# A two-model forward pass in float32: the dense feed-forwards with weight columns stationary

## The chip, the core and the metric

The kernel runs on one core of a Trainium2 chip. Five engines work side by side, each through its own instructions in order, and wait for one another by semaphores: TensorE (PE; its weight loads are listed apart as PEld), VectorE (DVE), ScalarE (ACT), GpSimd (POOL) and SyncE (SP), which here starts the weight transfers. The metric is the device time of one execution in microseconds (us). Before the change it is 2497.68 us, the median of three runs (2497.55 to 2498.68).

## What is computed

256 tokens of width 1024 go through two small models of two layers each. Every layer is a mixer (attention and recurrences, merged by gates) and a feed-forward. Three of the four feed-forwards are dense, with 2816 hidden channels; the last is a mixture of 8 experts. The change touches the dense ones alone:

```python
def rms_norm(x, g):
    xf = x.astype(jnp.float32)
    y = xf * lax.rsqrt(jnp.mean(xf * xf, axis=-1, keepdims=True) + NORM_EPS)
    return (y * g.astype(jnp.float32)).astype(x.dtype)

def swiglu(h, w_in, w_out):                  # layers 0 and 1 of the first model
    gate, up = jnp.split(h @ w_in, 2, axis=-1)
    return (jax.nn.silu(gate) * up) @ w_out
...
        h = rms_norm(x, ln2[l])
        x = x + swiglu(h, w_ffn_in[l], w_ffn_out[l])

def swiglu_2(h, w1, w3, w2):                 # layer 0 of the second model
    return (jax.nn.silu(h @ w1) * (h @ w3)) @ w2
```

## The kernel before

**Products in float32 out of rounded halves.** TensorE multiplies rounded numbers here (type fp32r). So each weight and each activation is split into its rounded value and the remainder, and a product is made of three: rounded by rounded, remainder of x by rounded weight, rounded x by remainder of the weight. All weights (616 MB) stream from memory in chunks of 128 x 2048 (1 MB). For every chunk ACT writes the rounded copy (`conv`, L1461, tile `w_hi`, a ring of 3 slots) and DVE the remainder (`conv`, L1917, tile `w_lo`, in place of the raw chunk, a ring of 6). PE counts `w_used` up when it is through with a chunk; ACT rounds chunk c only once chunk c-3 is used up, and SP fetches chunk c once chunk c-6 is.

**The dense feed-forward** (`feed_forward`) runs over J = 11 blocks of 256 hidden channels. A block takes three chunks: two for the up products (`up`, eight k tiles of 128 in two halves, each with 256 gate and 256 up columns) and one for the down product (`down`). In `up`, a k tile of x for 128 tokens is stationary and 512 weight columns move (`gemm_half`, L792 to L794: three products for each of 4 k tiles and 2 token tiles, 24 of 512 columns in a chunk). The result has tokens on the partitions: one of the eight PSUM banks for each token tile, gate columns left and up columns right. Blocks alternate between banks 0, 1 and banks 2, 3 (`gbank`). ACT takes the silu of the gate half (scaled per token by the norm's factor, column 4+t of `nstat`), DVE multiplies it by the up half (L2441, `gprod`). The down product contracts over hidden channels, which must then lie on the partitions, so PE turns `gprod` by four transposes of 128 x 128 for each block (`turn_block`, L774), ACT rounds the turned values (`ghi`) and DVE writes their remainder (L2449, `glo`). The down products of all blocks add up in banks 4 to 7, called X.

**The order.** `walk` gives the order for each engine: first up of block 0 (both halves), up of block 1 (first half), turn of block 0, up of block 1 (second half), down of block 0; then for each further block: up (first half), turn of the block before, up (second half), down of the block before. The middle blocks are a hardware loop. In block j = J-2, the last block's turn stands in the middle of the down product.

**The start of a feed-forward.** Before it, the mixer's output product adds up in banks 0 to 3: banks 0 and 1 hold columns 0 to 511 of the update of x, banks 2 and 3 the rest. DVE adds them to x (`add_to_x`, L1952) and so sets them free: 0 and 1 while PE still makes the second half, 2 and 3 after its end. PE transposes x in four norm tiles into the X banks (L774 `x`); ACT rounds them (`xhi`), DVE makes the remainders (L1936, `xlo`). Tiles 0 and 1 are transposed before the first up product, tiles 2 and 3 in its middle (`rest_of_norm`), since they need the second half of x. ACT sums the squares (`hrow`), and computes the factor of the norm only after it has rounded the next chunk (`scale`: two table loads, a logarithm and an exponential).

**Lines to follow**: `up` with `gemm_half` (L792 to L794), `turn_block` (L774), `down` with `gemm_rows` (L807 to L809), `add_to_x` (L1952), `lo_tiles` (L1936), `conv` of ACT (L1461) and of DVE (L1917).

## Time and profile before

| | us |
|---|---|
| median of three runs | 2497.68 |
| the profiled execution | 2497.54 |
| its span, first to last instruction | 2495.9 |
| PE busy with products | 2472.0 (99%) |
| DVE busy | 1814.5 (73%) |
| ACT busy | 1523.7 (61%) |

Busy time of PE is the union of records that overlap: a record of 512 columns lasts 0.39 us, but one starts every 0.227 us, and it is this distance that counts. Shapes in a row are partitions x elements; `x4` counts instructions that stand together. In a timeline, a row gives start, duration, engine, line, operation, and in brackets how long the engine sat idle before it and who ended that.

### The profile page before, as it was taken

Reading aid. Unit: us, or ns where it says so; the run is one execution under the profiler, and the core shown is the slowest. Engines: PE = TensorE matmul, PEld = TensorE weight load, DVE = VectorE, ACT = ScalarE, POOL = GpSimd, SP = SyncE. Lnnn points to the kernel's source line nnn. Section 1 sums busy time; section 2 is a strip of 40 time slices with the busy share of each in tenths; the row PEclk is TensorE's granted clock in tenths of the full one; section 3 lists DMA queues with packets and bytes.
Section 4 is the critical chain, followed back from the end, with each engine's and each line's share of the span. In section 5 each row is a group of like instructions: output and inputs, shape, how many; then the busy total and the mean of one; then the engine's idle time right before and its main releaser. Section 6 shows DMA issues by size and latency. Waiting matters only on the chain.

```text
span 2495.9 us, 31808 instructions
## 1 busy us (share of the span) xinstructions
PE 2472.0 (99%) x11756; PEld 2024.7 (81%) x11756; DVE 1814.5 (73%) x1839; ACT 1523.7 (61%) x1589; POOL 153.5 (6%) x133
## 2 busy tenths in 40 slices
PE   8999999999999999999999999999999999999998
PEld 7888888888888888888888887888888888888877
DVE  6687655657775555665556577989889898998988
ACT  6565544555554455545445546777777777777776
POOL 0102000020020000110000023000000000000010
PEclk9999999999999999999999999999999999999999
DMA  7445555544455564555554456999999999999996
GB/s 262 152 161 177 171 188 190 172 158 152 169 179 190 187 208 161 182 173 186 187 184 169 169 194 252 383 368 387 385 374 385 373 386 375 385 369 392 368 402 254
DMA packets 90684, 633.76 MB, mean 254 GB/s; under 512 B 10462, under 2 KB 10838, under 8 KB 15841
## 3 DMA queue, kind: packets, MB, share of 16 engines
q1 hardware_dynamic: 85584, 616.63, 66.9%
q0 software_dynamic: 4720, 15.57, 1.7%
q8 instruction: 60, 0.98, 0.2%
q10 hardware_dynamic: 288, 0.33, 0.0%
q14 instruction: 32, 0.25, 0.0%
HBM read 625.00 MB, written 7.48 MB: 253 GB/s over the span
## 4 chain that ended last, share of the span: by engine, by line
PE 96%; DVE 2%; ACT 1%; DMA 1%; issue 1%; SPq 0%; ACTq 0%; DVEq 0%
PE bank L792 13%; PE bank L794 13%; PE bank L793 13%; PE bank L1371 8%; PE bank L1373 8%; PE bank L1372 8%; PE bank L1344 4%; PE bank L1346 4%; PE bank L1345 4%; PE bank L774 4%; PE bank L807 4%; PE bank L809 4%; PE bank L808 4%; PE bank L1200 1%; PE bank L1201 1%; PE bank L1199 1%
## 5 line engine op out<-in xcount | busy, mean ns | idle before, releaser
L1917 DVE TENSOR_TENSOR w_lo<-raw,w_hi 128x2048 fp32r<-128x2048 f32 x583 | 1341.6, 2303 | 417.6 <-ACT w_hi L1461 405.5
L1461 ACT ACTIVATE w_hi<-raw 128x2048 fp32r<-128x2048 f32 (+1 forms) x588 | 1120.1, 1907 | 259.9 <-PE bank L809 117.3
L792 PE MATMUL bank<-w_hi,xhi 128*128 128x512 f32 x1456 | 579.9, 398 | 1.5 <-DVE w_lo L1917 0.7
L794 PE MATMUL bank<-w_lo,xhi 128*128 128x512 f32 x1456 | 567.9, 390 | 0.0
L793 PE MATMUL bank<-w_hi,xlo 128*128 128x512 f32 x1456 | 567.5, 390 | 0.0
L1371 PE MATMUL bank<-w_hi,xhi 128*128 128x512 f32 x896 | 358.8, 400 | 0.8 <-DVE w_lo L1917 0.5
L1373 PE MATMUL bank<-w_lo,xhi 128*128 128x512 f32 x896 | 350.0, 391 | 0.0
L1372 PE MATMUL bank<-w_hi,xlo 128*128 128x512 f32 x896 | 349.6, 390 | 0.0
L792 PEld LDWEIGHTS bank<-w_hi,xhi 128*128 128x128 f32 x1456 | 273.4, 188 | 66.3 <-issue 7.5
L794 PEld LDWEIGHTS bank<-w_lo,xhi 128*128 128x128 f32 x1456 | 273.3, 188 | 58.5
L793 PEld LDWEIGHTS bank<-w_hi,xlo 128*128 128x128 f32 x1456 | 273.7, 188 | 53.0
L1373 PEld LDWEIGHTS bank<-w_lo,xhi 128*128 128x128 f32 x896 | 168.2, 188 | 35.5
L1371 PEld LDWEIGHTS bank<-w_hi,xhi 128*128 128x128 f32 x896 | 168.3, 188 | 33.3 <-DVE w_lo L1917 1.3
L1461 ACT ACTIVATE ghi<-bank 128x256 fp32r<-128x256 f32 x178 | 65.0, 384 | 212.1 <-PE bank L774 212.1
L1372 PEld LDWEIGHTS bank<-w_hi,xlo 128*128 128x128 f32 x896 | 168.7, 188 | 31.4
L1344 PE MATMUL bank<-w_hi,ghi 128*128 128x512 f32 x448 | 175.4, 392 | 1.2 <-DVE glo L2526 1.1
L1346 PE MATMUL bank<-w_lo,ghi 128*128 128x512 f32 x448 | 174.5, 389 | 0.0
L1345 PE MATMUL bank<-w_hi,glo 128*128 128x512 f32 x448 | 174.3, 389 | 0.0
L807 PE MATMUL bank<-w_hi,ghi 128*128 128x512 f32 x264 | 103.5, 392 | 0.0
L809 PE MATMUL bank<-w_lo,ghi 128*128 128x512 f32 x264 | 102.8, 389 | 0.0
L808 PE MATMUL bank<-w_hi,glo 128*128 128x512 f32 x264 | 102.8, 389 | 0.0
L2783 POOL TENSOR_TENSOR u<-u,gates 128x512 f32<-128x512 f32 x32 | 61.2, 1944 | 655.0 <-DVE gates L2355 655.0
(371 smaller groups left out, 2307.2 us busy)
## 6 DMA issues: line engine op xcount, KB each, us to landing
raw<-in_wexpert SPq DMA_DIRECT2D x336, 1024.0 KB, 4.9
raw<-in_wdense SPq DMA_DIRECT2D x248, 1024.0 KB, 4.8
expert_rows<-y POOLq DMA_DIRECT2D x7, 512.0 KB, 4.8
expert_rows<-back POOLq DMA_DIRECT2D x3, 512.0 KB, 3.9
x<-in_x SPq DMA_DIRECT2D x2, 512.0 KB, 4.6
raw<-in_wdense SPq DMA_DIRECT2D x4, 256.0 KB, 6.1
biasT<-bias_rows POOLq DMA_DIRECT2D x1, 1024.0 KB, 6.3
normal_rows<-hnorm POOLq DMA_DIRECT2D x1, 1024.0 KB, 8.2
```

Of the source, the lines that this page charges most:

```text
L792: mm(bank[banks[t]][:, :], xhi[:, k0 + k, tok], wh, start=start and k == 0, stop=False)
L793: mm(bank[banks[t]][:, :], xlo[:, k0 + k, tok], wh, start=False, stop=False)
L794: last = mm(bank[banks[t]][:, :], xhi[:, k0 + k, tok], wl, start=False, stop=stop and k == 3)
L807: mm(b, xh, hi[:, h, o:o + 512], start=first and k == 0, stop=False)
L1344: mm(dst, ghi[:, m, j % 2, :], hi[:, h, w], start=first, stop=False)
L1345: mm(dst, glo[:, m, j % 2, :], hi[:, h, w], start=False, stop=False)
L1346: return mm(dst, ghi[:, m, j % 2, :], lo[:, s, w], start=False, stop=final)
L1371: mm(bank[b][:, :], xhi[:, kt, 0:P], hi[:, h, w], start=kt == 0, stop=False)
L1372: mm(bank[b][:, :], xlo[:, kt, 0:P], hi[:, h, w], start=False, stop=False)
L1373: last = mm(bank[b][:, :], xhi[:, kt, 0:P], lo[:, s, w], start=False, stop=kt == KT - 1)
L1461: return nc.scalar.activation(dst, src, f, **kw)
L1917: V.tensor_tensor(lo[:, c % RAW, :], raw[:, c % RAW, :], hi[:, c % HI, :].bitcast(F32), ALU.subtract).then_inc(lo_ready, 1)
```

## The change

The up products are turned round. A 128 x 128 piece of the weights is stationary, and the tokens move: the tiles `xhi` and `xlo` become the two halves of one tile `xboth`, so one product of the rounded weights sees 512 columns (256 tokens rounded, 256 tokens of remainders) and fills a whole bank, and a second product of the weights' remainder sees 256 columns and adds to the bank's left half. Four banks (gate and up, two pieces of 128 channels each) are one block, and all blocks use banks 0 to 3. The result is channel-major at once. The transposes are gone. The two halves of each bank are added by ACT (copy of the right half to `side`) and DVE (sum). The norm's factor is per token, now along the free axis: PE spreads it over the partitions once for each feed-forward (a product of ones with a diagonal, `diag`, into `rstd_row`), and DVE multiplies by it. ACT's silu, DVE's product, ACT's rounding and DVE's remainder follow, all of 128 x 256, out of SBUF.

```diff
-                        for t in range(NT):
-                            claim((k, "U", j), 2 * (j % 2) + t, streamed=True)
-                            claim((k, "T", j), 2 * (j % 2) + t)
+                        claim((k, "U", j), 0, 1, 2, 3, streamed=True)
+                    claim((k, "R"), X[3])
...
+                        kt, w = 4 * half + kk, slice(kk * 512 + (m % 2) * FB + m // 2 * P, kk * 512 + (m % 2) * FB + m // 2 * P + P)
+                        both = bank[m][:, :].rearrange("p (a b) -> p a b", a=2)
+                        if kt < KT - 1:
+                            mm(both, hi[:, h, w], xboth[:, :, kt, :], start=kt == 0, stop=False)
+                            return mm(bank[m][:, 0:S], lo[:, s, w], xhi[:, kt, :], start=False, stop=False)
+                        mm(bank[m][:, 0:S], lo[:, s, w], xhi[:, kt, :], start=False, stop=False)
+                        return mm(both, hi[:, h, w], xboth[:, :, kt, :], start=False, stop=True)
+
+                    if j == 0 and half == 0:
+                        for m in range(4):
+                            pe.wait_ge(free[m], use((k, "U", j), m))
+                        for kk in range(4):
+                            if kk == 2:
+                                rest_of_norm(k)
+                            for m in range(4):
+                                last = channels(m, kk)
+                    else:
+                        for m in range(4):
+                            if half == 0:
+                                pe.wait_ge(free[m], use((k, "U", j), m) + 2 * it)
+                            for kk in range(4):
+                                last = channels(m, kk)
+                            if half == 1 and m == 1:
+                                last.then_inc(first_block_done, 1)
+                    last.then_inc(w_used, 1)
+                    if j == 0 and half == 1:
+                        b = X[3]
+                        pe.wait_ge(free[b], use((k, "R"), b))
+                        pe.wait_ge(diag_ready, DENSE[k] + 1)
+                        for t in range(NT):
+                            last = mm(bank[b][:, t * P:t * P + P], C("ones"), diag[:, t, :], start=True, stop=True)
+                        last.then_inc(full[b], 1)
...
-                    for t in range(NT):
-                        b = gbank(j, t)
-                        pe.wait_ge(free[b], ev((k, "T", j), b) + 2 * it)
+                    pe.wait_ge(glo_done, FFB[k] + 2 * j + 2 + 4 * it)
```

ACT, after each block's up products:

```diff
                     conv(c0 + c + 2, it)
-                        go(silu[:, t, :], bank[gbank(j, t)][:, 0:FB], ACT.Silu, scale=nstat[:, 4 + t:5 + t]).then_inc(silu_done, 1)
+                    for m in range(2):
+                        if m == 0:
+                            act.wait_ge(first_block_done, FFB[k] // 2 + j + 1 + 2 * it)
+                        else:
+                            act.wait_ge(w_used, c0 + c + 1 + 6 * it)
+                        for i in (2 * m, 2 * m + 1):
+                            last = go(side[:, i, :], bank[i][:, S:2 * S], ACT.Copy)
+                        last.then_inc(side_ready, 1)
+                    for m in range(2):
+                        act.wait_ge(gate_scaled, FFB[k] + 2 * j + m + 1 + 4 * it)
+                        go(silu[:, m, :], silu[:, m, :], ACT.Silu).then_inc(silu_done, 1)
```

DVE, after each block's up products (`added` takes two sums out of the banks and frees them, `scaled` multiplies both by `rstd_row`; `products`, in the place of the turn, multiplies gate by up and writes the remainders):

```diff
                     conv(c0 + c + 2, it)
+                    added(0)
+                    if j > 0:
+                        scaled(0)
+                    added(1)
+                    if j == 0:
+                        b = X[3]
+                        wait_full((k, "R"), b)
+                        V.tensor_copy(rstd_row[:, :], bank[b][:, 0:S]).then_inc(free[b], 1)
+                        dve.wait_ge(free[b], ev((k, "R"), b))
+                        scaled(0)
+                    scaled(1)
+                    if j == J - 1:
+                        products(j, it)
```

The order on PE at the first up product of the first dense feed-forward, before and then after; `bank_freeN` is the semaphore by which bank N comes free, L792 and L1286 are the first up products, and `ident_t,x` is a norm transpose:

```order
L792 MATMUL bank<-w_hi,xhi 128x512 [waits bank_free1,lo_ready,bank_free0,bank_free4]
L793 MATMUL bank<-w_hi,xlo 128x512
L794 MATMUL bank<-w_lo,xhi 128x512
...
L774 MATMUL bank<-ident_t,x 128x128 [waits bank_free3,bank_free6,bank_free2,bank_free5]
L774 MATMUL bank<-ident_t,x 128x128 x3
L774 MATMUL bank<-ident_t,x 128x128 [waits bank_free7,bank_free3,bank_free2]
```

```order
L1286 MATMUL bank<-xboth,w_hi 128x512 [waits bank_free1,bank_free2,bank_free0,bank_free3,lo_ready,bank_free4]
L1287 MATMUL bank<-xboth,w_lo 128x256
L1286 MATMUL bank<-xboth,w_hi 128x512
...
L782 MATMUL bank<-ident_t,x 128x128 [waits bank_free3,bank_free6,bank_free2,bank_free5]
L782 MATMUL bank<-ident_t,x 128x128 x3
L782 MATMUL bank<-ident_t,x 128x128 [waits bank_free7,bank_free3,bank_free2]
```

The wait for banks 2 and 3 moved from the middle of the first up chunk to its first product.

The order on PE where block 1 begins, before and then after:

```order
L792 MATMUL bank<-w_hi,xhi 128x512 [waits lo_ready,bank_free3,bank_free2]
...
L774 MATMUL bank<-ident_t,gprod 128x128 [waits bank_free0]
L774 MATMUL bank<-ident_t,gprod 128x128
L774 MATMUL bank<-ident_t,gprod 128x128 [waits bank_free1]
L774 MATMUL bank<-ident_t,gprod 128x128
L792 MATMUL bank<-w_hi,xhi 128x512 [waits lo_ready]
```

```order
L1289 MATMUL bank<-xboth,w_hi 128x512
L1313 MATMUL bank<-diag,cst 128x128 [waits rstd_diagonal_ready,bank_free7]
L1313 MATMUL bank<-diag,cst 128x128
L1286 MATMUL bank<-xboth,w_hi 128x512 [waits bank_free0,lo_ready]
L1287 MATMUL bank<-xboth,w_lo 128x256
...
L1286 MATMUL bank<-xboth,w_hi 128x512 [waits bank_free1]
```

Block 1 waited for banks 2 and 3, which block 0 had not used; now it waits for banks 0 and 1, which block 0 has just filled.

The order on DVE over the same place, before and then after (L1917 and L1955 write the remainder of a weight chunk):

```order
L1917 TENSOR_TENSOR w_lo<-raw,w_hi 128x2048 [waits hi_ready] x2
L2441 SCALAR_TENSOR_TENSOR gprod<-bank,nstat,silu 128x256 [waits silu_done] x2
L1917 TENSOR_TENSOR w_lo<-raw,w_hi 128x2048 [waits hi_ready]
L2449 TENSOR_TENSOR glo<-bank,ghi 128x2x128 [waits gated_hi] x2
```

```order
L1955 TENSOR_TENSOR w_lo<-raw,w_hi 128x2048 [waits hi_ready]
L2524 TENSOR_SCALAR diag<-ident_t,nstat 128x128 [waits norm_rstd]
L2524 TENSOR_SCALAR diag<-ident_t,nstat 128x128
L1955 TENSOR_TENSOR w_lo<-raw,w_hi 128x2048 [waits hi_ready]
L2482 TENSOR_TENSOR silu<-bank,side 128x256 [waits remainder_products_out]
L2482 TENSOR_TENSOR gprod<-bank,side 128x256
L2482 TENSOR_TENSOR silu<-bank,side 128x256 [waits remainder_products_out]
L2482 TENSOR_TENSOR gprod<-bank,side 128x256
L2499 COPY rstd_row<-bank 128x256 [waits bank_full7]
```

The sums that free banks 0 and 1 stand behind the remainder of the chunk after next.

## Rows read from the trace of the kernel before

**Rows 1.** The page: busy time of the engines, and shares of the last chain.
```profile
PE 2472.0 (99%) x11756; PEld 2024.7 (81%) x11756; DVE 1814.5 (73%) x1839; ACT 1523.7 (61%) x1589; POOL 153.5 (6%) x133
PE 96%; DVE 2%; ACT 1%; DMA 1%; issue 1%; SPq 0%; ACTq 0%; DVEq 0%
```

**Rows 2.** Line L774 within 283:470 us: times are min/median/max in ns.
```profile
L774 PE MATMUL bank<-ident_t,gprod x44: 270/272/273, 293.4 to 453.5; 128*128 128x128 f32 x44
```

**Rows 3.** Timeline of PE, loop of the first dense feed-forward.
```profile
299.28 0.39 PE L807 MATMUL bank<-w_hi,ghi 128*128 128x512 f32 x1
...
304.72 0.39 PE L792 MATMUL bank<-w_hi,xhi 128*128 128x512 f32 x1
...
310.16 0.60 PE L774 MATMUL bank<-ident_t,gprod 128*128 128x128 f32 x4
310.52 0.47 PE L792 MATMUL bank<-w_hi,xhi 128*128 128x512 f32 x1
310.83 0.39 PE L793 MATMUL bank<-w_hi,xlo 128*128 128x512 f32 x1
...
450.41 0.39 PE L807 MATMUL bank<-w_hi,ghi 128*128 128x512 f32 x1
```

**Rows 4.** Timeline of PE, start of the first dense feed-forward.
```profile
275.61 0.49 PE L792 MATMUL bank<-w_hi,xhi 128*128 128x512 f32 x1
...
278.49 1.03 PE L774 MATMUL bank<-ident_t,x 128*128 128x128 f32 x8
279.28 0.47 PE L792 MATMUL bank<-w_hi,xhi 128*128 128x512 f32 x1
...
282.36 0.47 PE L792 MATMUL bank<-w_hi,xhi 128*128 128x512 f32 x1
```

**Rows 5.** Timeline of DVE there.
```profile
276.26 1.28 DVE L1952 TENSOR_TENSOR x<-bank,x 128x512 f32<-128x512 f32 x2
...
288.44 2.29 DVE L1917 TENSOR_TENSOR w_lo<-raw,w_hi 128x2048 fp32r<-128x2048 f32 x1 [3.02 <-ACT w_hi L1461]
...
294.61 0.75 DVE L2449 TENSOR_TENSOR glo<-bank,ghi 128x256 fp32r<-128x256 f32 x2
```

**Rows 6.** Timeline of ACT there.
```profile
279.75 1.55 ACT L1461 ACTIVATE xhi<-bank,par 128x256 fp32r<-128x256 f32 x4
...
286.49 1.92 ACT L1461 ACTIVATE w_hi<-raw 128x2048 fp32r<-128x2048 f32 x1
...
293.77 0.66 ACT L1461 ACTIVATE ghi<-bank 128x256 fp32r<-128x256 f32 x2 [1.40 <-PE bank L774]
```

**Rows 7.** Timeline of PE and DVE, the other two dense feed-forwards.
```profile
727.71 0.50 PE L792 MATMUL bank<-w_hi,xhi 128*128 128x512 f32 x1
...
1122.20 0.50 PE L792 MATMUL bank<-w_hi,xhi 128*128 128x512 f32 x1
...
728.35 1.28 DVE L1952 TENSOR_TENSOR x<-bank,x 128x512 f32<-128x512 f32 x2
```

**Rows 8.** Timeline of PE, products of 256 moving columns with 28 stationary ones.
```profile
16.65 0.28 PE L920 MATMUL bank<-xhi,wsm_hi 128*28 128x256 f32 x1
...
17.45 0.28 PE L921 MATMUL bank<-xlo,wsm_hi 128*28 128x256 f32 x1
```

**Rows 9.** Timeline of PEld, loads of 128 columns; L947 moves 256 columns, L948 128.
```profile
44.74 0.19 PEld L947 LDWEIGHTS bank<-tri,zs 128*128 128x128 f32 x1
44.85 0.19 PEld L948 LDWEIGHTS bank<-tri,zs 128*128 128x128 f32 x1
44.97 0.19 PEld L792 LDWEIGHTS bank<-w_hi,xhi 128*128 128x128 f32 x1
...
310.83 0.19 PEld L794 LDWEIGHTS bank<-w_lo,xhi 128*128 128x128 f32 x1
```

**Rows 10.** Windows (length, busy us of the engines, granted clock, DMA share, GB/s); PE's longest idle.
```profile
1525.00:1530.00 5.00, 3.55 (x20) 3.49 (x20) 3.81 (x22) 2.36 (x4) 1.88 (x4) 0.57 1.01 324
...
1524.58 0.36 PE L1438 MATMUL bank<-chosen,cst 128*128 128x8 f32 x2 [2.15 <-DVE chosen L2552]
```

More of the change, by code:

```diff
@@ L595, in program @@
         NEXT = dict(zip(phases, phases[1:]))
+        NORMS = {p: i for i, p in enumerate(p for p in phases if p[0] == "norm")}
+        DENSE = {p: i for i, p in enumerate(p for p in phases if p[0] in ("ffn1", "ffn2"))}
         def gated(j):
@@ L1269, in up @@
                             pe.wait_ge(free[X[i]], ev(("norm", k[1], k[0]), X[i]))
-                    banks = [gbank(j, t) for t in range(NT)]
-                    if half == 0:
-                        for b in banks:
-                            pe.wait_ge(free[b], use((k, "U", j), b) + 2 * it)
-                    gemm_half(banks, c0 + c, 4 * half, half == 0, half == 1, it,
-                              middle=(lambda: rest_of_norm(k)) if j == 0 and half == 0 else lambda: None)
-                def turn(j, it):
-                    if j < J - 1:
-                        turn_block(j, it)
@@ L1796, in up_done, with rounded @@
                     conv(c0 + c + 2, it)
[L1797 to L1799 removed]
+                    for m in range(2):
[10 more added lines that the diff above has]
+                    if j == J - 1:
+                        rounded(j, it)
+                def rounded(j, it):
+                    for m in range(2):
+                        act.wait_ge(product_ready, FFB[k] + 2 * j + m + 1 + 4 * it)
+                        go(gated(j)[0][:, m, :, :].rearrange("p t n -> p (t n)"), gprod[:, m, :], ACT.Copy).then_inc(ghi_done, 1)
                 def turn(j, it):
[L1802 to L1805 removed]
+                    if j < J - 1:
+                        rounded(j, it)
                 walk(act, J, lambda j, it, c: conv(c0 + c + 2, it) if c else None, turn, up_done, lambda j, it, c: conv(c0 + c + 2, it))
@@ L2452, in feed_forward, with added @@
-                walk(dve, J, lambda j, it, c: conv(c0 + c + 2, it), turn, up_done, down)
+                    def added(m):
+                        if f0 + 2 * j + m > 1:
+                            dve.wait_ge(glo_done, f0 + 2 * j + m - 1 + 4 * it)
+                        dve.wait_ge(side_ready, f0 + 2 * j + m + 1 + 4 * it)
+                        for i, dst in ((2 * m, silu), (2 * m + 1, gprod)):
+                            V.tensor_tensor(dst[:, m, :], bank[i][:, 0:S], side[:, i, :], ALU.add).then_inc(free[i], 1)
@@ new lines, in scaled @@
+                    def scaled(m):
+                        for i, dst in ((2 * m + 1, gprod), (2 * m, silu)):
+                            dve.wait_ge(free[i], ev((k, "U", j), i) + 2 * it)
+                            last = V.tensor_tensor(dst[:, m, :], dst[:, m, :], rstd_row[:, :], ALU.mult)
+                        last.then_inc(gate_scaled, 1)
+                    conv(c0 + c + 2, it)
+                    added(0)
+                    if j > 0:
+                        scaled(0)
+                    added(1)
@@ new lines, in up_done, with products @@
+                    if j == 0:
[5 more added lines that the diff above has]
+                    scaled(1)
+                    if j == J - 1:
+                        products(j, it)
+                def products(j, it):
+                    for m in range(2):
+                        dve.wait_ge(silu_done, f0 + 2 * j + m + 1 + 4 * it)
+                        V.tensor_tensor(gprod[:, m, :], gprod[:, m, :], silu[:, m, :], ALU.mult).then_inc(product_ready, 1)
+                    for m in range(2):
+                        dve.wait_ge(ghi_done, f0 + 2 * j + m + 1 + 4 * it)
+                        gh, gl = (part[:, m, :, :].rearrange("p t n -> p (t n)") for part in gated(j))
+                        V.tensor_tensor(gl, gprod[:, m, :], gh.bitcast(F32), ALU.subtract).then_inc(glo_done, 1)
@@ new lines, in turn, with up_begun @@
+                def turn(j, it):
+                    if j < J - 1:
+                        products(j, it)
+                def up_begun(j, it, c):
+                    conv(c0 + c + 2, it)
+                    if j == 0:
+                        dve.wait_ge(norm_rstd, NORMS["norm", k[1], k[0]] + 1)
+                        for t in range(NT):
+                            last = V.tensor_scalar(diag[:, t, :], ident_t[:, :], nstat[:, 4 + t:5 + t], None, ALU.mult)
+                        last.then_inc(diag_ready, 1)
@@ L2454, in pick_first @@
+                walk(dve, J, up_begun, turn, up_done, down)
             def pick_first():
```

40 lines of the change are left out of this document (13 added, 27 removed).

## The prediction

> **What bounds the kernel now.** I read the page first: PE is busy for 99% of the span and makes up 96% of the chain that ended last, DVE and ACT are at 73% and 61% [rows 1]. So time leaves the kernel only if PE gets fewer or closer products, and returns if PE waits. Next I read PE's timeline through the loop of a dense feed-forward. The reader is to see the distance between starts: the down product begins at 299.28 and the next chunk's up products at 304.72, so 24 products of 512 columns take 5.44 us, 0.227 each. The down product of the tenth block begins at 450.41; that is nine periods of (450.41 - 299.28) / 9 = 16.79 us [rows 3]. Three chunks at 5.44 make 16.32. The other 0.47 us is the turn: four transposes from 310.16 to 310.52, and a first product behind them that takes 0.31 before the next starts, with a few slightly longer ones after it [rows 3]. There are 44 transposes, 11 turns, in each feed-forward [rows 2], 33 turns in all three.
>
> **What goes.** All 33 turns. In the steady blocks that is 0.47 us each and nothing hides behind them, because PE has no idle time there. I count them by layer: 10 turns lie after the first down product, 10 x 0.47 = 4.7 us, three times 14.1 us. The first turn is inside the start, which I work out by itself.
>
> **What stays equal.** A chunk had 24 products of 512 columns. Now it has 16 of 512 and 16 of 256, the same 12288 columns. What is unknown is the distance that a 256-column product keeps with a full load of 128 columns behind it; the kernel before has none in steady flow. Lower bound: half of 0.227, 0.113. Near it lie the 256-column products with 28 stationary columns: seven from 16.65 to 17.45, 0.114 each [rows 8]. Upper bound: loads of 128 columns at 44.85 and 44.97, 0.12 apart around a 256-column product, in a stretch right after an interruption; the loads at 44.74 and 44.85, around a product of 128 columns, show that a load alone comes every 0.11 [rows 9]. A load of 0.11 just fits under a product of 0.113. I take 1.2 ns over the lower bound, nearer to the flowing row. There are 16 x 2 x 33 = 1056 such products: +1.3 us, with ends 0 and 1056 x 7.7 ns = +8.1 us. The load must lie beside the running product for this, and it does: the load for L794 and the product L793 both start at 310.83 [rows 3, 9]. The Trainium skill, TensorE: Matmul & The Clock Gate, section "Part 3: Packing small matmuls — row/col tiling", says that a weight load overlaps a running matmul only when the row group differs; here all loads and products use all rows, so the trace disagrees. By that rule the 528 extra loads at its P / 1.2 (an estimate from the page: 107 ns) would add 56 us.
>
> **What is added beside PE.** Each block, DVE now has four sums, four multiplications, two products and two remainders, six pairs. A pair of 256-column operations takes 0.75 us [rows 5], so 4.5 us, with three weight remainders of 2.29 11.4 us out of 16.3. ACT has four copies (two pairs of 0.66 [rows 6]), silu and rounding, 2.7 us, and three roundings of 1.92: 8.4 us. Neither is a bound. In steady flow I count from the start T of a block's second up chunk. DVE is through with the chunk's remainder at T+4.4, frees banks 0 and 1 by T+5.2, ACT's copies of the other two banks end at T+6.3, banks 2 and 3 are free at T+7.1, and PE wants bank 0 at T+10.9. Behind ACT's wait for the scaled gate stands the rounding of the next chunk but one: it starts at about T+8.3, its remainder is done at T+12.5 and PE wants it at T+16.3. In the last block, the chain from the end of the up products to the last remainder (copies, sums, scaling, silu, product, rounding, remainder) is about 4.2 us beside a down product of 5.44. So all of this is hidden, by 1.2 us at the tightest. If that cover is gone, PE pays the rest once a block.
>
> **What the start of a feed-forward costs.** Two waits are new, and each stands at the head of PE's queue, with all up products behind it.
>
> *First wait.* The first up product now wants banks 2 and 3, that is DVE's second sum into x. It ends at 276.26 + 1.28 = 277.54 [rows 5]; with 0.08 for the semaphore (an estimate; from ACT to DVE it is 0.03, 286.49 + 1.92 against 288.44 [rows 5, 6]) 277.62, where the kernel before starts at 275.61 [rows 4]. Before, six products of each token tile covered this. +2.0 us. The other layers give the same: 728.35 + 1.28 + 0.08 against 727.71, and in the third the start 1122.20 stands in the same place [rows 7].
>
> *Up to the second.* First half chunk 2.88 and norm transposes 0.79, as before [rows 4], then 12 products' worth with the restart behind the transposes, 12 x 0.227 + 0.11 = 2.83, then 5.44: PE is through with block 0 at 277.62 + 11.94 = 289.56. The kernel before begins this second chunk at 282.36, 3.08 after 279.28 [rows 4], 0.25 more than the products take, for it waits for the last tiles of x; ACT's sum of squares held them up (its rounding begins only at 279.75 [rows 6]), and with PE 2 us later it no longer does.
>
> *Second wait.* Block 1 wants bank 0, which DVE frees with its first sum. By the order that sum stands behind the remainder of the fourth chunk, which waits for ACT's rounding, which stands behind the norm's factor. ACT took up the last x tiles at 279.75 [rows 6]; now it can only when PE has transposed, 277.62 + 2.88 + 0.60 + 0.04 = 281.14, so everything behind slips by 1.39. The rounding at 286.49 becomes 287.88 [rows 6], the remainder at 288.44 becomes 289.83 and ends at 292.12 [rows 5], the sum ends at 292.46, and PE goes on at 292.54. That is 2.98 us after 289.56. The new product of ones with the diagonal lies inside this pause and costs nothing. Were the pause gone, it would cost at least two transposes' 0.22 [rows 3]; no row shows a plain float32 product of this shape alone, and I take 0.7 for both where it counts, in a rival.
>
> *Sum of the start.* Block 1 takes 10.88 and 0.11 for the restart (0.47 less the 0.36 of the transposes), so the first down product begins at 303.53 instead of 299.28 [rows 3]: +4.3 us a layer, 12.8 us for three. What is late next: the fourth chunk's successor. ACT rounds it only after silu, about 295.7 to 297.6, remainder at 299.9, wanted at 303.53; the gated remainders are ready at 301.5. No further wait.
>
> **Sum.** -14.1 + 12.8 + 1.3 = 0.0 us. The profiled execution took 2497.54, 1.6 over its span and 0.14 under the median, so I forecast 2497.5 us. No change, and not because little moves: some 15 us of PE work go, and about as much waiting comes in.
>
> **Rivals.**
> - *The short product is bound by its load* (slower). At the upper bound, 121 ns, the sum is +6.8 above the row's 1.3: 2504.4 us. It decides from about 118 ns on. For it speaks the 0.12 at 44.85 [rows 9], against it that longer distances follow every interruption, those of 512 columns too, and go away. 0.17.
> - *The second wait is not there* (faster). If the banks come free before PE is through with block 0, the first down product begins at 289.56 + 0.7 + 10.9 = 301.2, 1.9 us late instead of 4.3, and the time is 2497.5 - 3 x 2.4 = 2490.4 us. For it speaks that DVE sits idle for 3.02 us before 288.44, against it that this idle is just the wait for ACT [rows 5]. 0.10.
> - *The clock falls in the new pauses* (slower). In the window 1525 to 1530 the granted clock was 0.57 [rows 10], so part of it ran at 1.2 GHz, after PE had been idle for 2.15 us with only tiny products around. The Trainium skill (TensorE: Matmul & The Clock Gate, "HAM oscillation — how this bites in real kernels") warns of the same: a waiting array falls back. My pauses are 2.0 and 3.0 us but stand between dense chunks. The window lost (1 - 0.57) x 5 = 2.2 us; if each of the six pauses costs that, it is 2510.7, for the three long ones alone 2504.1. 0.06.
> - *ACT's or DVE's order loses a steady block* (slower). A chain 1.5 us longer than I count, in the loop or the last block, would stall PE; 0.3 us in each of 33 blocks gives 2507. 0.06.
> - *Loads are not hidden at all*: 2554 us, 0.01, by the row at 310.83.
> - *The forecast*: 0.60, its own range 2494.5 to 2501.
>
> A run of this kernel can be told from no change at about 0.2%, 5 us: under 2492.7 is faster, over 2502.7 slower. Faster: the second rival and a little, 0.13. Slower: the others, 0.27. Same: 0.60. The range runs from 2490.5, the faster rival, to 2506: it leaves out half of the third and fourth rival and what may lie beyond the second.
>
> **What the profile after would show.** In the loop, the down products 16.35 us apart (16.32 to 16.6) instead of 16.79, and PE never idle. The 256-column products 0.113 to 0.116 from the next start. At each start PE idle for 2.0 us on DVE's sum into x, then, 12 us later, for about 2.3 us behind the two products of ones, on DVE's first sum. From the first up product of the kernel before to the first down product, 23.67 us become about 27.9. Wrong would be a period over 16.6 or PE idle in the loop, a start without the second pause, or a granted clock under 1 near 278 or 292 us.

## The result, and the profile after

The changed kernel takes 2512.40 us, the median of four runs (2510.58 to 2513.35), against 2497.68 us. The ratio is 1.0057 with the interval 1.0045 to 1.0070: slower by about 0.6%, where I had forecast no change and a range up to 2506 us. The profiled execution took 2511.73 us, 14.2 more than the one of before, with a span of 2510.1.

The page of the changed kernel, the lines that answer to [rows 1]:

```profile
PE 2474.3 (99%) x12164; PEld 2043.3 (81%) x12164; DVE 1907.3 (76%) x2112; ACT 1570.0 (63%) x1721; POOL 151.9 (6%) x133
PE 94%; DVE 2%; ACT 2%; issue 1%; DMA 1%; SPq 0%; ACTq 0%; DVEq 0%
```

PE still makes the chain. Its busy time grew by 2.3 us and the span by 14.2, so some 12 us more are spent idle; that is about what the two forecast waits come to (13.0 us, below). But the 33 turns that went were 33 x 0.47 = 15.5 us of PE's work, and PE is busy for longer without them. So its products must have become slower, and the timeline of PE has to be read for distances. This is its timeline in the first dense feed-forward and at the start of the second, which answers to [rows 3, 4, 7] (start, duration, line, and in brackets the idle time and who ended it):

```profile
277.55 0.47 PE L1286 MATMUL bank<-xboth,w_hi 128*128 128x512 f32 x1 [2.07 <-DVE x L1990]
...
289.72 0.61 PE L1313 MATMUL bank<-diag,cst 128*128 128x128 f32 x4
...
292.58 0.47 PE L1286 MATMUL bank<-xboth,w_hi 128*128 128x512 f32 x1 [2.25 <-DVE silu L2482]
...
305.39 0.40 PE L815 MATMUL bank<-w_hi,ghi 128*128 128x512 f32 x1
...
310.84 0.39 PE L1286 MATMUL bank<-xboth,w_hi 128*128 128x512 f32 x1
...
322.11 0.40 PE L815 MATMUL bank<-w_hi,ghi 128*128 128x512 f32 x1
...
455.81 0.40 PE L815 MATMUL bank<-w_hi,ghi 128*128 128x512 f32 x1
...
734.55 0.47 PE L1286 MATMUL bank<-xboth,w_hi 128*128 128x512 f32 x1 [2.07 <-DVE x L1990]
```

The reader is to see four things. Both pauses stand where they were forecast: PE starts at 277.55 (forecast 277.62) and goes on at 292.58 (forecast 292.54). The up products of a steady block take 322.11 - 310.84 = 11.27 us, where I had counted 10.92. Those of block 1, behind the second pause, take 305.39 - 292.58 = 12.81, which is 1.54 more than a steady block. And the first down product lies 6.11 us later than before, at the tenth block's down product 455.81 - 450.41 = 5.40 are left [rows 3]. The last turn of before lay just behind that place and cost 0.47, so the first dense feed-forward is longer by 4.93 us. The next one confirms it: its first up product comes 734.55 - 727.71 = 6.84 us later than before [rows 7], which is 4.9 and the 1.9 of its own first pause. Three make 14.8, and 0.6 us are gained elsewhere.

The two pauses as the list of waits of the changed kernel has them (total, times, longest):

```profile
PE bank L1286 <- DVE silu L2482: 6.8, 3, 2.3
PE bank L1286 <- DVE x L1990: 6.2, 3, 2.1
```

All three feed-forwards have both, and nothing else waits in the loop. Why the second pause is there is seen on DVE and ACT at its place:

```profile
289.81 2.29 DVE L1955 TENSOR_TENSOR w_lo<-raw,w_hi 128x2048 fp32r<-128x2048 f32 x1 [1.71 <-ACT w_hi L1486]
...
292.01 0.42 DVE L2482 TENSOR_TENSOR silu<-bank,side 128x256 f32<-128x256 f32 x1
```

```profile
281.09 1.57 ACT L1486 ACTIVATE xboth<-bank,par 128x256 fp32r<-128x256 f32 x4 [1.38 <-PE bank L782]
...
287.85 1.92 ACT L1486 ACTIVATE w_hi<-raw 128x2048 fp32r<-128x2048 f32 x1
```

ACT takes up the last tiles of x at 281.09 (worked out: 281.14). The rounding and the remainder are later than in [rows 5, 6] by 1.36 and 1.37 us (worked out: 1.39), and the remainder keeps DVE from the sum that frees bank 0, which ends only at 292.43.

The distances in a steady block of the changed kernel, from PE's timeline:

```profile
328.60 0.40 PE L1286 MATMUL bank<-xboth,w_hi 128*128 128x512 f32 x1
328.84 0.28 PE L1287 MATMUL bank<-xboth,w_lo 128*128 128x256 f32 x1
328.95 0.40 PE L1286 MATMUL bank<-xboth,w_hi 128*128 128x512 f32 x1
...
329.66 0.40 PE L1286 MATMUL bank<-xboth,w_hi 128*128 128x512 f32 x1
```

Three pairs take 1.06 us, 0.353 each; three times 0.227 and 0.1145 would be 1.02. The short product costs 0.113 to 0.120, 0.117 on average, near what I took. The surprise is the long one: 0.232, 0.241 and 0.236 in turn instead of 0.227, with the same columns as before.

The windows of the changed kernel around the second pause of the three layers (length, then busy us and count of PE, PEld, DVE, ACT, POOL, then granted clock, DMA share, GB/s):

```profile
290.00:295.00 5.00, 2.75 (x13) 2.20 (x13) 4.96 (x10) 2.56 (x6) 0.00 (x0) 0.85 0.60 213
295.00:300.00 5.00, 5.00 (x25) 4.33 (x24) 2.71 (x3) 2.22 (x2) 0.00 (x0) 0.81 0.00 0
...
748.00:753.00 5.00, 3.43 (x14) 2.95 (x15) 4.18 (x10) 2.32 (x4) 0.00 (x0) 0.78 0.52 197
...
1148.00:1153.00 5.00, 3.98 (x15) 3.48 (x16) 3.62 (x10) 2.33 (x4) 0.00 (x0) 0.72 0.44 184
```

At 295 to 300 PE is busy throughout and still makes only 25 products, at a granted clock of 0.81: part of it ran at 1.2 instead of 2.4 GHz. (1 - 0.85) x 5 + (1 - 0.81) x 5 = 1.7 us of full speed are missing, which is near what block 1 is late by (1.54). The traced execution has these three falls. The mean granted clocks of the four executions lie between 0.995 (2513.35 us) and 0.997 (2510.58 us), so the number of falls is probably not the same in each.

### The profile page after: what moved, and what is told of

It reads as the page before. It is cut to its first block, busy times and chain, and to the rows that moved or that the text cites. A ratio compares the mean times of both kernels' runs of the same rounds, so it can differ in the third digit from the quotient of the medians.

```text
span 2510.1 us, 33126 instructions
## 1 busy us (share of the span) xinstructions
PE 2474.3 (99%) x12164; PEld 2043.3 (81%) x12164; DVE 1907.3 (76%) x2112; ACT 1570.0 (63%) x1721; POOL 151.9 (6%) x133
## 4 chain that ended last, share of the span: by engine, by line
PE 94%; DVE 2%; ACT 2%; issue 1%; DMA 1%; SPq 0%; ACTq 0%; DVEq 0%
PE bank L1286 8%; PE bank L800 8%; PE bank L1396 8%; PE bank L1398 8%; PE bank L1397 8%; PE bank L802 8%; PE bank L801 8%; PE bank L1287 4%; PE bank L1369 4%; PE bank L1371 4%; PE bank L1370 4%; PE bank L815 3%; PE bank L817 3%; PE bank L816 3%; PE bank L782 3%; PE bank L1289 1%
## 5 line engine op out<-in xcount | busy, mean ns | idle before, releaser
L1955 DVE TENSOR_TENSOR w_lo<-raw,w_hi 128x2048 fp32r<-128x2048 f32 x583 | 1341.2, 2303 | 407.4 <-ACT w_hi L1486 394.1
L800 PE MATMUL bank<-w_hi,xboth 128*128 128x512 f32 x928 | 370.8, 400 | 1.2 <-DVE w_lo L1955 0.7
L802 PE MATMUL bank<-w_lo,xboth 128*128 128x512 f32 x928 | 361.9, 390 | 0.0
L801 PE MATMUL bank<-w_hi,xboth 128*128 128x512 f32 x928 | 361.8, 390 | 0.0
L1396 PE MATMUL bank<-w_hi,xboth 128*128 128x512 f32 x896 | 358.8, 400 | 0.6 <-DVE w_lo L1955 0.3
L1398 PE MATMUL bank<-w_lo,xboth 128*128 128x512 f32 x896 | 350.1, 391 | 0.0
L1397 PE MATMUL bank<-w_hi,xboth 128*128 128x512 f32 x896 | 349.5, 390 | 0.0
L1286 PE MATMUL bank<-xboth,w_hi 128*128 128x512 f32 x924 | 335.9, 402 | 13.0 <-DVE silu L2482 6.8
L1287 PE MATMUL bank<-xboth,w_lo 128*128 128x256 f32 x924 | 261.0, 283 | 0.0
L1286 PEld LDWEIGHTS bank<-xboth,w_hi 128*128 128x128 f32 x924 | 175.9, 190 | 52.7 <-issue 7.5
L800 PEld LDWEIGHTS bank<-w_hi,xboth 128*128 128x128 f32 x928 | 174.2, 188 | 44.2 <-issue 6.0
L802 PEld LDWEIGHTS bank<-w_lo,xboth 128*128 128x128 f32 x928 | 174.1, 188 | 37.4
L801 PEld LDWEIGHTS bank<-w_hi,xboth 128*128 128x128 f32 x928 | 174.5, 188 | 33.5
L1398 PEld LDWEIGHTS bank<-w_lo,xboth 128*128 128x128 f32 x896 | 168.2, 188 | 35.5
L1396 PEld LDWEIGHTS bank<-w_hi,xboth 128*128 128x128 f32 x896 | 168.3, 188 | 33.4 <-DVE w_lo L1955 1.2
L1397 PEld LDWEIGHTS bank<-w_hi,xboth 128*128 128x128 f32 x896 | 168.7, 188 | 31.5
L1287 PEld LDWEIGHTS bank<-xboth,w_lo 128*128 128x128 f32 x924 | 176.6, 191 | 5.5
L1369 PE MATMUL bank<-w_hi,ghi 128*128 128x512 f32 x448 | 175.4, 392 | 0.6 <-DVE glo L2601 0.5
L1371 PE MATMUL bank<-w_lo,ghi 128*128 128x512 f32 x448 | 174.5, 389 | 0.0
```

Source lines behind the costliest of these rows:

```text
L800: mm(bank[banks[t]][:, :], xhi[:, k0 + k, tok], wh, start=start and k == 0, stop=False)
L801: mm(bank[banks[t]][:, :], xlo[:, k0 + k, tok], wh, start=False, stop=False)
L802: last = mm(bank[banks[t]][:, :], xhi[:, k0 + k, tok], wl, start=False, stop=stop and k == 3)
L1286: mm(both, hi[:, h, w], xboth[:, :, kt, :], start=kt == 0, stop=False)
L1287: return mm(bank[m][:, 0:S], lo[:, s, w], xhi[:, kt, :], start=False, stop=False)
L1369: mm(dst, ghi[:, m, j % 2, :], hi[:, h, w], start=first, stop=False)
```

## The experiments

Two questions were open: what makes long products slower beside short ones, and whether the clock really falls because of the pauses. Distances given in ns are differences between single starts that the trace records; rows, which put products of one line together, stand beside them.

### 1. Is it the moving operand in two pieces?

In the change, `xboth` has rounded values and remainders 10 x 256 elements apart, so a long product reads two pieces. The theory was that the short product disturbs the stream, the rival that the two pieces do. Laid side by side:

```diff
-        xboth = sb("xboth", [P, 2, 10, S], F32R)
+        xboth = sb("xboth", [P, 10, 2, S], F32R)
```

> Only the layout of the moving tile changes: xboth is [kt][rounded, remainder][256 tokens] instead of [rounded, remainder][kt][256], so the 512 moving columns of a product lie in one piece. In the changed kernel a pair (512 + 256 columns) takes 352 ns where 341 were forecast (up chunk pairs: 11.27 us for 32). Theory B, the moving operand in two pieces slows the product: pair back to 341, period of a block 16.71 -> 16.36, about -11 us, 2501 us. Theory A, the 256-column product leaves the next load too little room and the stream never regains its lead, and theory C, the change of length itself: no change, 2512 us, pair 352.

Measured: 2513.48 us, ratio 1.0064 (1.0047 to 1.0081). PE's timeline in this kernel:

```profile
333.66 0.40 PE L1286 MATMUL bank<-xboth,w_hi 128*128 128x512 f32 x1
333.90 0.28 PE L1287 MATMUL bank<-xboth,w_lo 128*128 128x256 f32 x1
334.02 0.40 PE L1286 MATMUL bank<-xboth,w_hi 128*128 128x512 f32 x1
```

Nothing changed: a long one still keeps 0.24 (333.66 to 333.90), and the period of a block is 16.713 us as in the changed kernel. The rival (theory B) falls.

### 2. Is it each change of length?

Four long products in a row, then four short ones, instead of taking turns:

```diff
+                        parts = [(kk, True) for kk in kks] + [(kk, False) for kk in kks]
+                        if half == 1:
+                            parts = [(kk, False) for kk in kks] + [(kk, True) for kk in kks]
```

> Within a bank and a chunk the four 512-column products come first and then the four of 256 (the other way round in the second half), instead of in turn. Theory C, each change between lengths costs: 8 changes become 2, the chunk of 16 + 16 products goes from 5.63 to about 5.49 us, -9 us in all. Theory A, each load behind a 256-column product is late by some 5 ns and the 512-column products are slow only because the lead is lost: 512s regain 227 after one or two, 256s stay at 117 to 120, chunk about 5.53 us, -6 us in all. Theory B: every 512-column product stays at 235, no change.

Measured: 2510.88 us, ratio 1.0050 (1.0034 to 1.0067). PE's timeline:

```profile
333.47 1.09 PE L1295 MATMUL bank<-xboth,w_hi 128*128 128x512 f32 x4
334.40 0.63 PE L1296 MATMUL bank<-xboth,w_lo 128*128 128x256 f32 x4
334.87 1.09 PE L1295 MATMUL bank<-xboth,w_hi 128*128 128x512 f32 x4
```

Four long ones take 0.93 us, 0.2325 each, and four short ones 0.47: a pair costs 0.350, hardly less than 0.353. It isn't mainly paid per change of length (theory C), for three quarters of the changes are gone. Theory A was too hopeful as well: the long ones are not back at 227 ns after one or two of them. Of the 9 and 6 us that the two had promised, 1.5 came. In layer 2 the clock fell behind the first pause too, which it didn't do in the trace of the changed kernel:

```profile
735.00:740.00 5.00, 5.00 (x28) 4.50 (x27) 1.15 (x2) 2.13 (x7) 0.00 (x0) 0.77 0.21 85
```

### 3. Without short products

This kernel leaves out the up products with the weights' remainder, so all products are long; what is left is the pure stream of the new orientation.

```diff
-                            mm(both, hi[:, h, w], xboth[:, :, kt, :], start=kt == 0, stop=False)
-                            return mm(bank[m][:, 0:S], lo[:, s, w], xhi[:, kt, :], start=False, stop=False)
...
+                        return mm(both, hi[:, h, w], xboth[:, :, kt, :], start=kt == 0, stop=kt == KT - 1)
```

> Leaves out the up products with the weights' remainder in the dense feed-forwards (the 256-column ones), so all up products are of 512 columns with weights stationary and the two-piece moving tile. Theory B: they stand 235 ns apart. Theories A and C: 227 ns apart, because nothing short lies between them. The period of a block falls by about a third of the up part or to what DVE and ACT need (about 12.7 us); its spacing is read where PE doesn't wait.

Measured: 2463.93 us in one run. PE now outruns the chunks and waits for DVE's remainders 44.1 us in all, so the total says nothing about the price; the timeline does:

```profile
326.81 3.92 PE L1285 MATMUL bank<-xboth,w_hi 128*128 128x512 f32 x16 [1.75 <-DVE w_lo L1951]
330.67 0.49 PE L815 MATMUL bank<-w_hi,ghi 128*128 128x512 f32 x1
```

Behind a pause, it takes 3.86 us from the first of 16 long products to the down product, instead of 16 x 0.227 = 3.63. The starts are 335, 231, 236, 228, 233, 231, 226 and 227 ns apart, and 227 from then on, but for the last: the down product comes 325 behind it, which is a short stop in front of that one and no price of the stream. So long products in the new orientation do keep 227 ns, but only once some six of them have run in a row. Before that they are nearly as slow as the changed kernel's long products always are.

### 4. Short products in the kernel before

The reverse: the old orientation, its third product cut into two short ones, with nothing else changed.

```diff
-                        last = mm(bank[banks[t]][:, :], xhi[:, k0 + k, tok], wl, start=False, stop=stop and k == 3)
+                        mm(bank[banks[t]][:, 0:256], xhi[:, k0 + k, tok], wl[:, 0:256], start=False, stop=False)
+                        last = mm(bank[banks[t]][:, 256:512], xhi[:, k0 + k, tok], wl[:, 256:512], start=False, stop=stop and k == 3)
```

> The kernel before, where the third product of gemm_half (weights' remainder, 512 columns) is cut into two of 256 with the same stationary x: 512, 512, 256, 256. The moving operands lie in one piece everywhere. Theories A and C: the 512-column products beside the short ones slow down from 227 to 230-240 ns in steady flow and the 256s take 117-120, a dense block's chunk of 5.44 us becomes about 5.6 us. Theory B: 227 and 113 ns, the chunk stays at 5.44 us and the time at 2498 us.

Measured: 2516.44 us in one run, 18.6 over the kernel before, measured beside it (2497.82). PE's timeline, the first product of a group of four, and that of the third group after it:

```profile
327.18 0.40 PE L792 MATMUL bank<-w_hi,xhi 128*128 128x512 f32 x1
...
329.27 0.40 PE L792 MATMUL bank<-w_hi,xhi 128*128 128x512 f32 x1
```

Three groups take 2.09 us, so one of 1536 columns takes 0.697 instead of 0.681. The two long products of the first are 233 and 236 ns apart from what follows, the short ones 116 and 112. There is no pause and no fall of the clock at the starts here. So the price belongs to short products in a stream with a load for each, and doesn't need the new orientation. No run has short products without a load for each, so whether it is the product or its load isn't shown.

### 5. The second wait taken away

In block 0, ACT copies banks 0 and 1 before it rounds the fourth chunk, and DVE adds them before that chunk's remainder:

```diff
-                    conv(c0 + c + 2, it)
-                    added(0)
+                    if j == 0:
+                        added(0)
+                        conv(c0 + c + 2, it)
+                    else:
+                        conv(c0 + c + 2, it)
+                        added(0)
```

> At block 0 of each dense feed-forward alone, ACT copies the remainders of banks 0 and 1 before it rounds the fourth chunk, and DVE takes the two sums that free these banks before that chunk's remainder. In the changed kernel PE idles 2.25 us there and the granted clock is 0.5 for 3.41 us right after, which costs about 1.55 us. My theory, the pause is what lets the clock fall: both go, 3 x (2.2 + 1.55) = -11 us, 2501 us. Rival, the clock falls for the low activity of the start as a whole (the first pause of 2.07 us stays): only the wait goes, -6.6 us, 2506 us.

Measured: 2502.58 us, ratio 1.0019 (1.0010 to 1.0029). PE's timeline, then a window there:

```profile
289.73 0.61 PE L1313 MATMUL bank<-diag,cst 128*128 128x128 f32 x4
290.09 0.47 PE L1286 MATMUL bank<-xboth,w_hi 128*128 128x512 f32 x1
...
301.58 0.40 PE L815 MATMUL bank<-w_hi,ghi 128*128 128x512 f32 x1
```

```profile
290.00:295.00 5.00, 5.00 (x30) 4.24 (x30) 4.63 (x8) 2.55 (x5) 0.00 (x0) 1.00 0.61 213
```

Both the pause and the fall of the clock are gone here, and the first down product comes 3.81 us earlier. Three times that is 11.4, but only 9.8 came, as one fall (about 1.5) is left. In layer 2 the clock now fell behind the *first* pause, which it had not done in the changed kernel:

```profile
730.00:735.00 5.00, 4.15 (x15) 3.61 (x16) 2.90 (x3) 2.19 (x4) 0.00 (x0) 0.66 0.49 200
```

### 6. The pause kept, but filled

Is it idleness that lets the clock fall? Eight long products whose result nobody reads run inside the second pause:

```diff
+                        for _ in range(8):
+                            mm(bank[b][:, :].rearrange("p (a b) -> p a b", a=2), xhi[:, 0, 0:P], xboth[:, :, 1, :], start=True, stop=True)
                         pe.wait_ge(diag_ready, DENSE[k] + 1)
```

> Eight products of 512 columns, whose result nothing uses, are put into the second pause of each dense feed-forward (after the second up chunk of block 0, into the bank of the norm's factor, which is overwritten behind them). They take 1.8 us of the 2.9 us that PE is waiting there, so no other instruction moves. Idle theory: the clock stays up at all three places, -4.6 us against the changed kernel, about 2508 us. If the clock falls for another reason (first pause, kind of products): no change, 2512 us.

Measured: 2511.51 us, ratio 1.0050 (1.0033 to 1.0067), where the theory of the pause wanted some 4.6 us less than the changed kernel. The windows and PE's timeline show why:

```profile
275.00:280.00 5.00, 2.92 (x11) 2.18 (x10) 4.72 (x7) 2.56 (x6) 0.00 (x0) 0.81 0.60 210
280.00:285.00 5.00, 5.00 (x29) 4.47 (x29) 1.41 (x4) 2.28 (x5) 0.00 (x0) 0.85 0.00 0
290.00:295.00 5.00, 4.58 (x26) 3.84 (x25) 3.56 (x6) 3.78 (x6) 0.00 (x0) 1.00 0.48 162
...
735.00:740.00 5.00, 5.00 (x25) 4.38 (x24) 1.80 (x1) 2.10 (x5) 0.00 (x0) 0.66 0.37 154
...
1135.00:1140.00 5.00, 5.00 (x25) 4.43 (x24) 1.30 (x1) 2.10 (x6) 0.00 (x0) 0.67 0.22 92
```

```profile
277.67 0.47 PE L1286 MATMUL bank<-xboth,w_hi 128*128 128x512 f32 x1 [2.08 <-DVE x L1992]
...
294.21 0.47 PE L1286 MATMUL bank<-xboth,w_hi 128*128 128x512 f32 x1 [0.41 <-DVE silu L2484]
```

Behind the filled pause the clock stays at 1.00, as the theory said. But now it falls behind the first pause, in all three layers, and that costs the same. My expectation of the total missed. Either pause of about 2 us can bring the fall; in the trace of the changed kernel only the second did, here only the first. What decides I can't say: 2.07 us of idle is followed by 1.00 in one trace and 2.08 by 0.81 in another, although up to that first pause of layer 1 PE has the same instructions in both, since the eight products come 12 us later. So it isn't the instructions alone. In the traces of the changed kernel and of experiments 1, 2, 5 and 6, the clock fell behind all 9 pauses of 2.23 to 2.25 us, and behind 5 of the 15 of 2.07 to 2.09.

### 7 and 8. Both waits taken away

To experiment 5 is added that banks 0 and 1 take k tiles 0 and 1 first, so that banks 2 and 3 are wanted some 1.5 us later (7); and that with the order of experiment 2 (8).

```diff
+                            if m % 2 == 0:
+                                for i in (m, m + 1):
+                                    pe.wait_ge(free[i], use((k, "U", j), i))
+                            for kk in range(2):
+                                channels(m, kk)
+                        rest_of_norm(k)
```

> e5 and in addition the first wait halved: in the first up half chunk, banks 0 and 1 get their k tiles 0 and 1 before PE waits for banks 2 and 3. Of the 2.07 us pause 0.6 should stay, and the transposes of x come 1.45 us earlier, so the rest of the start moves up by as much: -1.4 us a layer against e5, about 2497 us. If ACT's and DVE's chain sets the start and not PE, -0.5 us a layer at most, 2500 us.

> e7 with the grouping of e2 (four products of 512 columns, then four of 256, in a bank and chunk). e2 measured about 2 us less than the changed kernel; the effects add up, since one is spacing and the other waits: 2 us under e7, about 2495 us, which would be the first version under the kernel before by 2 to 3 us (0.1%). If the spacing gain came from the clock's phase and not from the grouping, it equals e7.

Measured: 2496.74 us, ratio 0.9994 (0.9984 to 1.0004), and 2495.33 us, ratio 0.9989 (0.9979 to 0.9998). The order of experiment 2 gave 1.4 us, for 2 expected. PE's timeline in experiment 7:

```profile
277.62 0.47 PE L1286 MATMUL bank<-xboth,w_hi 128*128 128x512 f32 x1 [0.39 <-DVE x L1996]
...
300.15 0.47 PE L815 MATMUL bank<-w_hi,ghi 128*128 128x512 f32 x1
```

Without the pauses the clock stays at 1.00 through every start, and the first down product is only 0.87 us later than before. What is left is the balance of the loop, the turns against the price of the short products, and it is near nothing. A period is 16.713 us instead of the 16.32 of three chunks without it, so 27 periods pay 27 x 0.393 = 10.6: -14.1 + 3 x 0.87 + 10.6 = -0.9, measured -1.3 (2496.74 against 2498.07 beside it).

### 9. All long ones first, then all short ones

If six long products are needed to get back to 227 ns, short ones should stand together. The first chunk of a block has its 16 long ones first, the second its 16 short ones (block 0's first chunk excepted):

```diff
+                        for whole in (half == 0, half == 1):
+                            for m in range(4):
...
+                                for kk in range(4):
+                                    last = channel(m, kk, whole)
```

> e8, but over all four banks of a chunk: in a block's first up chunk 16 products of 512 columns and then 16 of 256, in the second chunk 16 of 256 and then 16 of 512, so a block has one stretch of 32 short products and one of 56 long ones (16 + 24 of the down product + 16). Lead theory (a short product costs some 5 ns once the lead is gone, and some six long ones in a row at 233 bring it back): two up chunks take 10.88 + 32 x 0.0055 + 0.04 = 11.09 us instead of e8's 11.195, 33 x 0.1 = -3.5 us against e8, 2492 us, and long products outside the first six stand 227 ns apart. If each short product costs the same wherever it stands and long ones are slow for another reason, the chunks stay at 11.2 us and the time at 2495 us.

Measured: 2495.48 us, ratio 0.9993 (0.9984 to 1.0002). PE's timeline of a block in the loop, and of block 1:

```profile
318.24 0.39 PE L815 MATMUL bank<-w_hi,ghi 128*128 128x512 f32 x1
...
323.68 3.79 PE L1295 MATMUL bank<-xboth,w_hi 128*128 128x512 f32 x16
327.31 4.00 PE L1296 MATMUL bank<-xboth,w_lo 128*128 128x256 f32 x32
331.14 3.82 PE L1295 MATMUL bank<-xboth,w_hi 128*128 128x512 f32 x16
334.80 0.39 PE L815 MATMUL bank<-w_hi,ghi 128*128 128x512 f32 x1
```

```profile
292.25 2.11 PE L1295 MATMUL bank<-xboth,w_hi 128*128 128x512 f32 x8 [1.19 <-DVE silu L2494]
```

The first 16 long ones, behind long ones, take 3.63 us = 16 x 0.227. The 32 short ones take 3.83: the first is 113 ns, the others 120. The 16 long ones behind them take 3.66: 234, 236, 228, 232, 231, 227 and then 227. So the loss of this order is told completely: about 7 ns for each of the 31 short products after the first, 0.21 us, and 0.03 us for the first few long ones behind them. The up products take 11.12 instead of 11.27 us, and the period is 16.56. The total doesn't show it (2492 were expected), for in block 1 bank 2 is now wanted earlier and PE waits 1.19 us for it, in three layers. The granted clock stays at 1.00 behind this pause.

### 10. The same without the new pause

Block 0 keeps bank by bank in its second chunk, ACT copies all four banks, and DVE adds and scales them all, before either turns to the fourth chunk.

```diff
+                    elif j == 0:
+                        for m in range(4):
+                            last = channels(m, (0, 1, 2, 3))
...
+                    if j == 0:
+                        conv(c0 + c + 2, it)
                     for m in range(2):
```

> e9 with its one new pause taken away. In e9 PE idles 1.19 us in block 1 of each dense feed-forward: with all long products first it wants bank 2 after 8 products, while DVE takes the sums of banks 2 and 3 only behind the fourth chunk's remainder. Here block 0 keeps the bank by bank order in its second chunk, and at block 0 ACT copies all four remainders and DVE takes all four sums, the factor's copy and the four scalings before the fourth chunk's rounding and remainder. The steady blocks stay at 16.55 us. If the pause goes and nothing takes its place: 3 x 1.2 = -3.6 us, 2492 us, 0.2% under the kernel before. If the fourth chunk's remainder is then late (wanted some 5.6 us after PE leaves block 0, done by about 5.5): no gain over e9, 2495 us.

Measured: 2491.26 us, ratio 0.9973 (0.9963 to 0.9984). PE's timeline:

```profile
277.60 0.70 PE L1295 MATMUL bank<-xboth,w_hi 128*128 128x512 f32 x2 [0.41 <-DVE x L2007]
...
288.35 0.61 PE L1327 MATMUL bank<-diag,cst 128*128 128x128 f32 x4
288.71 3.90 PE L1295 MATMUL bank<-xboth,w_hi 128*128 128x512 f32 x16
...
299.93 0.39 PE L815 MATMUL bank<-w_hi,ghi 128*128 128x512 f32 x1
```

PE idles 0.41 us here, goes from block 0 to block 1 without a pause, and the first down product is 0.65 later than before [rows 3]. The loop is that of experiment 9, with a period of 16.56 for 16.79: nine of them give back 2.1 us, and the last turn 0.47. By layer that is 0.65 - 2.1 - 0.47 = -1.9 us, -5.8 in all; the median lies 7.1 under that of the kernel before beside it (2498.32). This version beats the kernel before by 0.27% (interval 0.16 to 0.37%) and the changed one by 0.8%.

## Why the prediction was wrong

- **What goes**: right. Each period lost its turn of 0.47 us, the last one too (5.40 us became 4.93).
- **First wait**: right, 1.9 us for 2.0, PE at 277.55 for 277.62.
- **Second wait**: right in place, cause and length, 292.58 for 292.54, in all three layers.
- **The chains of DVE and ACT beside PE**: right. PE has no wait in the loop or in the last block.
- **The loads beside the running product**: right; 2554 us did not come.
- **What stays equal**: this is the step that failed. I priced one product, the short one, at 1.2 ns over half a long one, +1.3 us in all with an upper end of 8.1, and let the long ones keep 0.227. Measured is a period of 150.42 / 9 = 16.713 us for a forecast of 16.36, 0.353 a block, and 0.32 in blocks 0 and 1: 3 x (9 x 0.353 + 0.32) = 10.5 us on top of the 1.3. It lies beyond my upper end because that end, too, charged the short products alone. The row that I called nearer, seven products at 0.114 [rows 8], has only 28 stationary columns; the farther one, 0.12 with 128 of them [rows 9], is what short products in a row keep (experiment 9), and I had put it aside since "longer distances follow every interruption, and go away". They go away with some six long products; where every second product is short they never do. So my first rival (0.17) had the right place and the wrong size: over the steady blocks of the changed kernel the short products stand 117 ns apart on average, 4 over the half of a long one, and the long ones beside them 235, 8 over their 227, a cost that no case of the prediction had. I had even read the same thing off the turns of before ("a few slightly longer ones after it") and counted it as theirs.
- **The clock falls in the new pauses**: I gave it 0.06. In the traced execution it came in all three layers, 3 x 1.54 = 4.6 us, each fall at 0.7 of the row's 2.2 us. By itself it would have left the time inside my range. Against it I had only that dense chunks stand around the pause, which is no evidence. The Trainium skill (TensorE: Matmul & The Clock Gate, "HAM oscillation — how this bites in real kernels") warns that matmuls interrupted by waits fall back to the slow clock; here the trace agrees, with 0.85 and 0.81 behind a pause of 2.25 us, though not behind every pause (1.00 behind 2.07).

Together, for a layer: by the forecast the start is 4.25 us longer, nine periods are shorter by 0.43 each and the last turn by 0.47, which makes -0.1; plus 3.2 (nine periods), 0.3 (blocks 0 and 1) and 1.54 (the clock) it is 4.9, as measured. The forecast's "no change" was two terms of some 14 us against each other, so a term put down at 1.3 us that is really 12 decided the sign.

Shown are the price of short products (experiments 3, 4 and 9) and that filling or removing the pause keeps the clock behind it (5, 6, 7). Open is what inside TensorE a short product uses up and a long one gives back: loads can come every 0.11 us [rows 9], which alone would fit under 0.113, but in experiment 9 they come every 0.120, as the short products do. Open is also why the clock falls behind one pause and not behind another as long.

## What to carry to other kernels

When a stream of products changes its lengths, price the stream and not the product: look in the trace for the distances *of the neighbours* of the new form, and how many long products it takes until they are normal again. Keep short products together, away from the long ones: 32 in one row cost 0.24 us a block here, in turns with long ones 0.39. When a wait before the first product of a phase can't be avoided, look whether the bank that it waits for can be asked for later, and count a possible fall of the clock with every pause of some 2 us.

## What I had not expected of the hardware

- With new weights of 128 columns for each product, 512 moving columns take 227 ns in flow, but 228 to 236 until some six of them have run in a row after a stop or a short product (experiments 3 and 9), and 235 on average in turns with short ones; 256 columns take 113 once and then 120 each (experiment 9). The Trainium skill (TensorE: Matmul & The Clock Gate, "Back-to-back issue gap") gives N / 2.4 + 2.5 ns for one product, by which a pair would take 216 + 109 = 325 ns (an estimate from that formula), and 131 ns as a sustained distance at 512 columns; here a pair takes 353 at a granted clock of 1.00, and the shortest distance behind a product of 512 columns is 224.
- Two products of ones with a diagonal, float32 and 128 x 128, stand in the trace as four records and take 0.36 us (289.73 to 290.09 in experiment 5), the same as four transposes; I had assumed 0.7.
- Behind the pauses of 0.36 to 0.42 us and of 1.19 us at the starts (experiments 6 to 10) the granted clock stayed at 1.00; in the traces of the changed kernel and of experiments 1, 2, 5 and 6 it fell behind 5 of 15 pauses of 2.07 to 2.09 us, and behind all 9 of 2.23 to 2.25.
